# Token sums of three norms and a layer norm through a ones matrix held as weights, with root and inverse over all tokens in PSUM

## The chip, the core and the metric

One Trainium2 chip, one of its cores. A time is the device time of one execution in microseconds (us). The kernel before ran three times: 1002.34, 1003.82 and 1004.71 us, median 1003.82 us.

## What is computed

A decoder trunk of one layer over 512 prompt tokens and 64 sample tokens, 576 in all, with a model width of 1024. Cut to what matters here:

```python
x = x + HALF * gt1 * _swiglu(_rmsnorm(x, g_ffn1) * (1 + sc1) + sh1, w_ffn1_up, w_ffn1_down)      # norm 0
hm = _rmsnorm(x, g_mix) * (1 + scm) + shm                                                        # norm 1
proj = hm @ w_in
...
v = jax.nn.silu(_layernorm(v, ln_g, ln_b))                                                       # layer norm, width 512
...
x = x + gtm * (jnp.concatenate([v, p], axis=-1) @ w_out)
x = x + HALF * gt2 * _swiglu(_rmsnorm(x, g_ffn2) * (1 + sc2) + sh2, w_ffn2_up, w_ffn2_down)      # norm 2
return _rmsnorm(x)                                                                               # final norm

def _rmsnorm(x, g):
    return x * lax.rsqrt(jnp.mean(x * x, axis=-1, keepdims=True) + EPS) * g
```

## The kernel before

Activations lie transposed: 128 channels on the partitions, tokens along a row. `x` has 8 such chunks (`KD`) of 576 tokens (`TOKENS`); a row is treated as two halves of 288 tokens (`HALF`), each half holding 256 prompt and 32 sample tokens, and one half fills part of one PSUM bank. Every product is done in three passes of a value split in a high and a low part (`x_hi`, `x_lo`, `w_hi`, `w_lo`). Weights come in units of 1 MB; ScalarE (ACT) makes the high part of a unit, GpSimd (POOL) the low part, TensorE (PE) multiplies, VectorE (DVE) adds the result to `x`. Every engine's program is written out by hand in the order in which it runs, and semaphores are the only link between them. An instruction that waits holds up all that stands behind it on its engine.

A norm needs, for each token, the sum over 1024 channels of the squares of `x`, its root and inverse, and that inverse in all 128 partitions. Before the change this is done so:

- `square` (L1173) on ACT squares a chunk, `add_square` (L1582, L1585) on DVE adds the first seven into `acc` (a half of the tile `mean_ab`). The eighth square stays by itself in `sq[:, 1, :]`, and in norms 1 and 2 it is made in two halves (`last_square`, L1179 and L1181), since the last output tile of the stage before ends in two halves (`last_tile`, L611, with `last_residual` on DVE, L1877 to L1883, after each half).
- `token_sums` (L823) on PE takes 128 tokens of `acc` or `sq` as weights and one column of ones as the moving operand: 5 matmuls of one column for a row of 576 tokens. The sums of 128 tokens stand down the partitions, in five columns of `stat_ps`.
- `root` (L1222) on ACT and `inverse` (L1589) on DVE work on these 5 columns, in the SBUF tile `rms`.
- `spread` (L831) on PE, called by `norm_spread`, turns each column back into a row and copies it to all partitions (5 transposes of a broadcast column), into `stat_ps`, 576 columns (`r_ps`).
- `apply_norm` on DVE multiplies `x` by it: for each chunk `scale_samples` (L1610), a 512 column product with the gain (L1628) and two small ones. ACT then adds the shift (L1231) and makes `x_hi` (L1235); `x_lo` is made by DVE (L1615, even chunks) and POOL (L2167, odd ones). PE consumes these chunks one by one in `unit_chunk` (L711).

The layer norm is alike: means are taken away on DVE after a ones matmul (`ln_sum`, L977: weights are a 128 by 128 matrix of ones, and the 288 tokens of a half are the moving operand), ACT squares the four chunks of `v` (L1521), DVE adds three (L2119), PE sums (L823), ACT takes the root (L1523), DVE the inverse (L2121), PE spreads, DVE scales `v` (L2124), ACT applies Silu (L1533) and makes `x_hi` (L1529), and PE takes chunks 4 to 7 of unit OUT.

PE's program around these places: at the start a run of 68 transposes without use (`keep_warm`, L894), the sums, `first_products(0)` (L906), the spread, `first_turn(0)` (L915), and then unit 0 chunk by chunk. In norms 1 and 2 the sums of `acc` stand in the middle of the last half tile, the sums of the eighth square after it, with 8 and 6 transposes without use (`fillers`, L839) between, then the spread, then `ada_products` (L561; norm 1 has `ada_turn(4)` too), and the first unit chunk by chunk. In the layer norm the spread stands between chunks 2 and 3 of unit OUT, with `ada_products(7, 0, 1)` behind it.

`ada_products` reads weight quarters that DMA brings; the one that norm 2 waits for is issued by ACT behind the eighth square. On DVE `inverse(n)` stands behind `last_residual`; in norm 1 `mod_evacuate(4)` (L1559, L1572) stands between `inverse` and `apply_norm`. `final_norm` has its own helpers and keeps its own way.

## Time and profile before

| | |
|---|---|
| median of 3 runs | 1003.82 us |
| profiled execution, its own time | 1002.35 us |
| its span | 1000.6 us |
| PE busy | 987.4 us (99%) |
| DVE busy | 666.3 us (67%) |
| ACT busy | 525.4 us (53%) |
| POOL busy | 595.9 us (60%) |
| granted TensorE clock, mean of the span | 0.994 |

The profile is of one execution. The span is the time from the first instruction to the last; the profiled execution took 1.75 us more than its span. A granted clock of 1.00 is 2.4 GHz, of 0.50 it is 1.2 GHz. Matmuls overlap, so the time between the starts of two rows says more than a row's own duration.

### The profile page before, as it was taken

What the parts mean: (1) busy time and instruction counts of PE and PEld (TensorE: products, weight loads), DVE (VectorE), ACT (ScalarE), POOL (GpSimd) and SP (SyncE); (2) the same over time, 40 slices, a digit from 0 to 9 for tenths busy, and PEclk for the clock granted to TensorE, in tenths of its full rate; (3) what the DMA queues carried; (4) which work ended last, traced back from release to release, by engine and by line L of the source; (5) the groups of instructions that cost most, each with busy time, mean ns of one, the idle gap of its engine ahead of it and who ended that gap; (6) DMA issues with size and microseconds to landing.
All of it is one profiled execution on the core that took longest, in us unless ns stands there. A gap on an engine that the chain in (4) does not pass through costs nothing.

```text
span 1000.6 us, 19940 instructions
## 1 busy us (share of the span) xinstructions
PE 987.4 (99%) x7592; PEld 949.6 (95%) x7592; DVE 666.3 (67%) x1341; ACT 525.4 (53%) x957; POOL 595.9 (60%) x497
## 2 busy tenths in 40 slices
PE   8999999999999999999999999999999999999997
PEld 7799999999999998989977898999999999999996
DVE  3787766676666644369996537966776667666464
ACT  5756554556644542373365337656545666455432
POOL 2267666677776563346887133676766777656551
PEclk9999999999999999999999999999999999999998
DMA  9922322232224328744224631232223222232212
GB/s 365 366 86 88 124 84 86 87 123 86 85 86 169 126 85 301 269 164 191 85 34 183 238 127 44 84 110 102 85 85 107 105 86 84 88 124 85 98 72 95
DMA packets 22716, 127.51 MB, mean 127 GB/s; under 512 B 4192, under 2 KB 7392, under 8 KB 8032
## 3 DMA queue, kind: packets, MB, share of 16 engines
q1 hardware_dynamic: 19744, 105.28, 29.2%
q10 hardware_dynamic: 2880, 20.97, 5.5%
q8 instruction: 61, 1.00, 0.4%
q14 instruction: 31, 0.25, 0.1%
HBM read 123.06 MB, written 3.19 MB: 126 GB/s over the span
## 4 chain that ended last, share of the span: by engine, by line
PE 94%; POOL 2%; ACT 1%; DVE 1%; issue 1%; DMA 0%; POOLq 0%; DVEq 0%; ACTq 0%
PE tile_a L736 22%; PE tile_b L736 22%; PE ada_ps L736 18%; PE tile_a L589 10%; PE tile_b L589 8%; PE tile_a L711 2%; PE ada_ps L561 2%; PE tile_b L711 2%; PE tile_b L611 1%; PE tile_a L894 1%; POOL last_taps L2325 1%; PE stat_ps L823 1%; PE ada_ps L906 1%; PE tile_a L963 1%; PE tile_b L648 1%
## 5 line engine op out<-in xcount | busy, mean ns | idle before, releaser
L2181 POOL TENSOR_TENSOR w_lo<-w_raw,w_hi 128x512 fp32r<-128x512 f32 x168 | 217.0, 1298 | 106.7 <-ACT w_hi L1078 106.2
L2181 POOL TENSOR_TENSOR w_lo<-s_raw,w_hi 128x512 fp32r<-128x512 f32 x112 | 146.4, 1308 | 66.7 <-ACT w_hi L1078 66.7
L1078 ACT ACTIVATE w_hi<-w_raw 128x512 fp32r<-128x512 f32 x168 | 104.7, 625 | 63.8 <-PE ada_ps L736 50.2
L2145 POOL TENSOR_TENSOR w_lo<-w_raw,w_hi 128x2048 fp32r<-128x2048 f32 x16 | 73.6, 4597 | 93.6 <-ACT w_hi L1053 90.6
L736 PE MATMUL tile_a<-x_hi,w_hi 128*128 128x288 f32 x400 | 118.5, 296 | 0.0
L736 PE MATMUL tile_b<-x_hi,w_hi 128*128 128x288 f32 x400 | 118.4, 296 | 0.0
L736 PE MATMUL tile_b<-x_lo,w_hi 128*128 128x288 f32 x400 | 118.0, 295 | 0.0
L736 PE MATMUL tile_a<-x_lo,w_hi 128*128 128x288 f32 x400 | 118.0, 295 | 0.0
L736 PE MATMUL tile_b<-x_hi,w_lo 128*128 128x288 f32 x400 | 117.6, 294 | 0.0
L736 PE MATMUL tile_a<-x_hi,w_lo 128*128 128x288 f32 x400 | 117.6, 294 | 0.0
L736 PE MATMUL ada_ps<-x_hi,w_hi 128*128 128x288 f32 x320 | 94.8, 296 | 0.0
L736 PE MATMUL ada_ps<-x_lo,w_hi 128*128 128x288 f32 x320 | 94.4, 295 | 0.0
L736 PE MATMUL ada_ps<-x_hi,w_lo 128*128 128x288 f32 x320 | 94.1, 294 | 0.0
L2219 POOL TENSOR_TENSOR h_lo<-sq,h_hi 128x288 fp32r<-128x288 f32 x64 | 52.9, 847 | 38.3 <-ACT h_hi L1153 38.3
L736 PEld LDWEIGHTS tile_b<-x_hi,w_lo 128*128 128x128 f32 x400 | 75.3, 188 | 0.0
L736 PEld LDWEIGHTS tile_a<-x_hi,w_lo 128*128 128x128 f32 x400 | 75.3, 188 | 0.0
L736 PEld LDWEIGHTS tile_a<-x_lo,w_hi 128*128 128x128 f32 x400 | 75.1, 188 | 0.0
L736 PEld LDWEIGHTS tile_b<-x_lo,w_hi 128*128 128x128 f32 x400 | 75.1, 188 | 0.0
L736 PEld LDWEIGHTS tile_a<-x_hi,w_hi 128*128 128x128 f32 x400 | 74.9, 187 | 0.1
L736 PEld LDWEIGHTS tile_b<-x_hi,w_hi 128*128 128x128 f32 x400 | 74.9, 187 | 0.0
L1078 ACT ACTIVATE w_hi<-s_raw 128x512 fp32r<-128x512 f32 x112 | 70.0, 625 | 1.7 <-PE tile_a L736 1.7
L1125 ACT ACTIVATE full<-ada_ps 128x288 f32<-128x288 f32 x40 | 16.5, 411 | 95.0 <-PE ada_ps L736 95.0
(320 smaller groups left out, 2976.4 us busy)
## 6 DMA issues: line engine op xcount, KB each, us to landing
w_raw<-w_units SPq DMA_DIRECT2D x78, 1024.0 KB, 4.8
ada_lo<-w_ada SPq DMA_DIRECT2D x16, 1024.0 KB, 7.8
ada_lo<-w_ada ACTq DMA_DIRECT2D x14, 1024.0 KB, 7.5
ada_hi<-w_ada ACTq DMA_DIRECT2D x6, 1024.0 KB, 6.1
x<-x_in SPq DMA_DIRECT2D x4, 576.0 KB, 5.9
y_out<-x SPq DMA_DIRECT2D x8, 288.0 KB, 2.3
conv_s<-conv_state SPq DMA_DIRECT2D x1, 480.0 KB, 11.0
conv_s_out<-conv_s SPq DMA_DIRECT2D x1, 480.0 KB, 4.5
```

Source lines behind the costliest of these rows:

```text
L561: mm = pe.matmul(ada_bank(s)[32 * g:32 * g + 32, 0:ADA_N], cond[:, k, :], ada_slot(a)[:, kk, ADA_N * g:ADA_N * (g + 1)], start=(k == 0), s ...
L589: mm = pe.matmul(ps[:, h, 0:HALF], w[:, w_slot, cols], r(k, h), start=(first and n == 0), stop=(last and n == 2))
L611: mm = pe.matmul(tile_b[:, h, 0:HALF], w[:, u % 2, cols], t(k, h), start=(k == 0 and i == 0), stop=(k == kc - 1 and i == 2))
L648: mm = pe.matmul(tile_b[:, h, 0:HALF], w[:, u % 2, cols], t(k, h), start=(k == 0 and i == 0), stop=(k == n - 1 and i == 2))
L711: mm = pe.matmul(tiles[t][:, h, 0:HALF], w[:, u % 2, cols], r(k, h), start=(k == 0 and n == 0), stop=(k == KD - 1 and n == 2))
L736: mm = pe.matmul(ps, slot(w, i)[:, P * k:P * (k + 1)], r, start=(first and n == 0 and k == 0), stop=(n == 2 and k == KH - 1), skip_group_c ...
L823: mm = pe.matmul(out[:, j:j + 1], part[:, begin:begin + P], ones[:, 0:1], start=(first and j == 0), stop=(last and j == TOKEN_BLOCKS - 1))
L1078: nc.scalar.activation(slot(w_hi, i), source, ACT.Copy).then_inc(ready, 1)
L1125: nc.scalar.activation(gate_c22[:, 0, :], bank_a(u), ACT.Silu).then_inc(c11_gate, 1)
L2145: nc.gpsimd.tensor_tensor(w_lo[:, side, :], w_raw[:, side, :], w_hi[:, side, :].bitcast(F32), ALU.subtract).then_inc(w_lo_ready, 1)
L2181: return nc.gpsimd.tensor_tensor(slot(w_lo, i), raw, slot(w_hi, i).bitcast(F32), ALU.subtract)
L2219: nc.gpsimd.tensor_tensor(h_slot(h_lo, kk, x_slot), t1_raw[:, n - 1, :], h_slot(h_hi, kk, x_slot).bitcast(F32), ALU.subtract).then_inc(ht_ ...
```

## The change

`token_sums`, `spread`, `norm_spread` and the tile `rms` go. `row_sums` is new: the weights are the ones matrix, the moving operand is a half row of `acc` or `sq`, and the result is the sum of each of 288 tokens, already in all 128 partitions, in the half's bank of `stat_ps`. The root and the inverse are taken in place there: 288 columns for each half in the norms, 2 by 288 in one instruction in the layer norm. In norms 1 and 2 the sum of the first half of the eighth square stands before the last three matmuls of the last half tile, and its root stands on ACT between the two halves of that square. `column_sums` keeps the 8 fillers and the 6 fillers stay; the final norm stays as it is. Semaphore counts are renumbered for it. The two small slots that `sample_ps` uses move to columns 288 to 415 of their bank.

```diff
@@ last_tile (PE)
                         if h and k == kc // 2:
                             partial_sums(n)
+                        if h and k == kc - 1:
+                            pe.wait_ge(sq_half_ready, n)
+                            row_sums(sq[:, 1, :], 0, False, True).then_inc(stat_done, 1)
@@ partial_sums, column_sums and the helpers (PE)
                 pe.wait_ge(sq_used, (KD - 1) * (n + 1))
-                token_sums(sums_ps, acc, True, False)
+                row_sums(acc, 0, True, False)
+                row_sums(acc, 1, True, False)
 
             def column_sums(n):
                 if n == 0:
                     partial_sums(0)
+                    pe.wait_ge(sq_ready, KD)
+                    row_sums(sq[:, 1, :], 0, False, True).then_inc(stat_done, 1)
                 else:
-                    pe.wait_ge(sq_half_ready, n)
-                    token_sums(sums_ps, sq[:, 1, :], False, False, 0, 2)
                     if n < 3:
                         fillers(n, 8)
-                pe.wait_ge(sq_ready, KD * (n + 1))
-                token_sums(sums_ps, sq[:, 1, :], False, True, 2 if n else 0).then_inc(stat_done, 1)
-
-            def token_sums(out, part, first, last, begin_block=0, end_block=TOKEN_BLOCKS):
-                for j in range(begin_block, end_block):
-                    begin = min(P * j, TOKENS - P)
-                    mm = pe.matmul(out[:, j:j + 1], part[:, begin:begin + P], ones[:, 0:1],
-                                   start=(first and j == 0), stop=(last and j == TOKEN_BLOCKS - 1))
-                return mm
-
-            def spread(out=r_ps):
-                for j in range(TOKEN_BLOCKS):
-                    first = max(0, P * (j + 1) - TOKENS)
-                    mm = pe.transpose(out[:, P * j:P * (j + 1) - first],
-                                      rms[first:, 1, j:j + 1].broadcast_to([P - first, P]), ident[first:, first:])
-                return mm
+                    pe.wait_ge(sq_ready, KD * (n + 1))
+                row_sums(sq[:, 1, :], 1, False, True).then_inc(stat_done, 1)
+
+            def row_sums(part, h, first, last):
+                return pe.matmul(stat_ps[:, h, 0:HALF], ones[:], part[:, HALF * h:HALF * (h + 1)], start=first, stop=last)
...
-            def norm_spread(n):
-                pe.wait_ge(ident_ready, 1)
-                if n in (1, 2):
-                    fillers(n, 6)
-                pe.wait_ge(rstd_ready, n + 1)
-                spread().then_inc(r_ready, 1)
@@ layer norm (PE)
             pe.wait_ge(ln_sq_ready, CONV_CHUNKS)
-            token_sums(sums_ps, four[-1], True, False)
+            row_sums(four[-1], 0, True, False)
+            row_sums(four[-1], 1, True, False)
             ada_products(6, 3)
             pe.wait_ge(ln_sq_added, CONV_CHUNKS - 2)
-            token_sums(sums_ps, acc, False, True).then_inc(ln_var_mm, 1)
+            row_sums(acc, 0, False, True)
+            row_sums(acc, 1, False, True).then_inc(ln_var_mm, 1)
             out_chunk(2)
-            pe.wait_ge(ln_rstd_ready, 1)
-            spread().then_inc(ln_r_ready, 1)
             ada_products(7, 0, 1)
@@ last_square and root (ACT); norm 0 calls root(0, 0) and root(0, 1), norm() calls root(n, 1)
                 nc.scalar.activation(sq[:, 1, 0:HALF], x[:, KD - 1, 0:HALF], ACT.Square).then_inc(sq_half_ready, 1)
+                root(n, 0)
                 act.wait_ge(x_ready, NORM_TILES[n])
...
-            def root(n):
-                act.wait_ge(stat_done, n + 1)
-                nc.scalar.activation(rms[:, 0, :], sums_ps, ACT.Sqrt, scale=1.0 / D_MODEL,
+            def root(n, h):
+                act.wait_ge(stat_done, 2 * n + h + 1)
+                nc.scalar.activation(stat_ps[:, h, 0:HALF], stat_ps[:, h, 0:HALF], ACT.Sqrt, scale=1.0 / D_MODEL,
                                      bias=eps).then_inc(std_ready, 1)
@@ inverse and apply_norm (DVE)
             def inverse(n):
-                dve.wait_ge(std_ready, n + 1)
-                nc.vector.reciprocal(rms[:, 1, :], rms[:, 0, :]).then_inc(rstd_ready, 1)
+                for h in range(2):
+                    dve.wait_ge(std_ready, 2 * n + h + 1)
+                    nc.vector.reciprocal(stat_ps[:, h, 0:HALF], stat_ps[:, h, 0:HALF]).then_inc(rstd_ready, 1)
...
-                dve.wait_ge(r_ready, n + 1)
-                r = by_half(r_ps)
+                dve.wait_ge(rstd_ready, 2 * n + 2)
+                r = rows_ps
@@ layer norm (ACT, then DVE)
-            nc.scalar.activation(rms[:, 0, :], sums_ps, ACT.Sqrt, scale=1.0 / D_CONV, bias=eps).then_inc(ln_std_ready, 1)
+            nc.scalar.activation(rows_ps, rows_ps, ACT.Sqrt, scale=1.0 / D_CONV, bias=eps).then_inc(ln_std_ready, 1)
...
-            nc.vector.reciprocal(rms[:, 1, :], rms[:, 0, :]).then_inc(ln_rstd_ready, 1)
-            dve.wait_ge(ln_r_ready, 1)
+            nc.vector.reciprocal(rows_ps, rows_ps).then_inc(ln_rstd_ready, 1)
+            dve.wait_ge(ln_rstd_ready, 1)
             for c in range(CONV_CHUNKS):
-                nc.vector.tensor_tensor(v[:, c, :], v[:, c, :], r_ps, ALU.mult).then_inc(ln_scaled, 1)
+                nc.vector.tensor_tensor(by_half(v[:, c, :]), by_half(v[:, c, :]), rows_ps, ALU.mult).then_inc(ln_scaled, 1)
```

How the order moves on PE at the end of the first feed-forward stage, where norm 1 begins (`tile_b` is the last half tile, `ones` the ones, `mean_ab` holds `acc`, `ident` the identity). Before:

```order
2643 L611 MATMUL tile_b<-h_hi,w_hi 128x288
2644 L611 MATMUL tile_b<-h_lo,w_hi 128x288
2645 L611 MATMUL tile_b<-h_hi,w_lo 128x288
2646 L823 MATMUL stat_ps<-ones,sq 128x1 x2
2647 L839 MATMUL tile_a<-ident 128x128 x8
2648 L823 MATMUL stat_ps<-ones,sq 128x1 x3
2649 L571 MATMUL ada_ps<-ident,ada_rows 128x128 x2
2650 L839 MATMUL tile_a<-ident 128x128 x6
2651 L831 MATMUL stat_ps<-ident,rms 128x128 x4
2652 L831 MATMUL stat_ps<-ident,rms 128x64
2653 L561 MATMUL ada_ps<-ada_hi,cond 32x256 x8
```

And with the change:

```order
2641 L819 MATMUL stat_ps<-sq,ones 128x288
2642 L610 MATMUL tile_b<-h_hi,w_hi 128x288
2643 L610 MATMUL tile_b<-h_lo,w_hi 128x288
2644 L610 MATMUL tile_b<-h_hi,w_lo 128x288
2645 L825 MATMUL tile_a<-ident 128x128 x8
2646 L819 MATMUL stat_ps<-sq,ones 128x288
2647 L567 MATMUL ada_ps<-ident,ada_rows 128x128 x2
2648 L825 MATMUL tile_a<-ident 128x128 x6
2649 L557 MATMUL ada_ps<-ada_hi,cond 32x256 x8
```

One sum of the eighth square now stands ahead of the last three matmuls of the tile, and no spread stands between the fillers and `ada_products`.

On DVE at the same place, with the instruction behind the inverse (`mod`, `gain` belong to `mod_evacuate(4)`, `stat_ps<-x,stat_ps` is the first of `apply_norm`). Before:

```order
513 L1883 TENSOR_TENSOR x<-tile_b,x 128x32
514 L1589 RECIPROCAL rms<-rms 128x5
515 L1559 TENSOR_TENSOR mod<-ada_ps,vec 128x4x9 x2
516 L1572 SCALAR_TENSOR_TENSOR gain<-mod,vec 128x72
517 L1610 TENSOR_TENSOR stat_ps<-x,stat_ps 128x64
```

With the change:

```order
513 L1865 TENSOR_TENSOR x<-tile_b,x 128x32
514 L1571 RECIPROCAL stat_ps<-stat_ps 128x288 x2
515 L1540 TENSOR_TENSOR mod<-ada_ps,vec 128x4x9 x2
516 L1553 SCALAR_TENSOR_TENSOR gain<-mod,vec 128x72
517 L1592 TENSOR_TENSOR stat_ps<-x,stat_ps 128x64
```

The order is the same; what stands in place 514 is two instructions of 288 columns for one of 5.

## Rows read from the trace of the kernel before

**Rows 1.** The page: busy time by engine, and the chain that ended last
```profile
PE 987.4 (99%) x7592; PEld 949.6 (95%) x7592; DVE 666.3 (67%) x1341; ACT 525.4 (53%) x957; POOL 595.9 (60%) x497
...
PE 94%; POOL 2%; ACT 1%; DVE 1%; issue 1%; DMA 0%; POOLq 0%; DVEq 0%; ACTq 0%
```
**Rows 2.** Instructions on the tiles rms and rms_end: duration in ns, min/median/max
```profile
L1589 DVE RECIPROCAL rms<-rms x3: 189/189/189, 16.2 to 605.1; 128x5 f32<-128x5 f32 x3
...
L1904 DVE RECIPROCAL rms_end<-rms_end x2: 176/177/178, 987.5 to 991.4; 128x3 f32<-128x3 f32 x2
```
**Rows 3.** Groups by line and shape: busy us, mean ns | idle before
```profile
L1125 ACT ACTIVATE full<-ada_ps 128x288 f32<-128x288 f32 x40 | 16.5, 411 | 95.0 <-PE ada_ps L736 95.0
L1760 DVE TENSOR_TENSOR sil<-full,tile_b 128x288 f32<-128x288 f32 x28 | 12.7, 454 | 10.1 <-PE tile_b L736 10.1
```
**Rows 4.** Timeline of PE, layer norm: start us, us, instruction
```profile
532.75 4.10 PE L977 MATMUL stat_ps<-v,ones 128*128 128x288 f32 x16
...
542.77 1.17 PE L823 MATMUL stat_ps<-ones,sq 128*128 128x1 f32 x10
...
547.69 0.80 PE L831 MATMUL stat_ps<-ident,rms 128*128 128x128 f32 x5
...
551.26 0.51 PE L711 MATMUL tile_a<-x_hi,w_hi 128*128 128x288 f32 x2
```
**Rows 5.** Timeline of ACT and DVE, layer norm
```profile
546.19 0.27 ACT L1523 ACTIVATE rms<-stat_ps,small 128x5 f32<-128x5 f32 x1 [4.53 <-PE stat_ps L823]
...
550.22 0.69 ACT L1529 ACTIVATE x_hi<-full 128x576 fp32r<-128x576 f32 x1
...
548.53 2.75 DVE L2124 TENSOR_TENSOR v<-v,stat_ps 128x576 f32<-128x576 f32 x4 [1.85 <-PE stat_ps L831]
```
**Rows 6.** Timeline of norm 1: PE, ACT, DVE
```profile
430.31 0.50 PE L711 MATMUL tile_a<-x_hi,w_hi 128*128 128x288 f32 x2 [0.74 <-ACT x_hi L1235]
...
424.81 0.45 ACT L1181 ACTIVATE sq<-x 128x288 f32<-128x288 f32 x1 [2.82 <-DVE x L1883]
...
424.60 0.18 DVE L1883 TENSOR_TENSOR x<-tile_b,x 128x32 f32<-128x32 f32 x1
...
427.81 0.23 DVE L1610 TENSOR_TENSOR stat_ps<-x,stat_ps 128x64 f32<-128x64 f32 x1 [0.71 <-PE stat_ps L831]
```
**Rows 7.** Norm 2: timeline of PE and DVE, then the chain of waits
```profile
609.30 0.54 PE L711 MATMUL tile_a<-x_hi,w_hi 128*128 128x288 f32 x2
...
603.21 0.18 DVE L1883 TENSOR_TENSOR x<-tile_b,x 128x32 f32<-128x32 f32 x1
...
606.27 0.23 DVE L1610 TENSOR_TENSOR stat_ps<-x,stat_ps 128x64 f32<-128x64 f32 x1 [0.94 <-PE stat_ps L831]
...
603.43 4.82 DMA ada_lo<-w_ada
```
**Rows 8.** Timeline of norm 0, all engines
```profile
15.88 0.25 ACT L1222 ACTIVATE rms<-stat_ps,small 128x5 f32<-128x5 f32 x1
...
18.09 0.23 DVE L1610 TENSOR_TENSOR stat_ps<-x,stat_ps 128x64 f32<-128x64 f32 x1 [1.74 <-PE stat_ps L831]
...
18.80 0.23 DVE L1594 TENSOR_SCALAR mod<-ada_ps,vec 128x9 f32<-128x9 f32 x1 [0.47 <-PE ada_ps L915]
...
21.81 0.53 PE L711 MATMUL tile_a<-x_hi,w_hi 128*128 128x288 f32 x2
```
**Rows 9.** Table by stretch: us, busy (x) of PE, PEld, DVE, ACT, POOL, granted clock, DMA, GB/s
```profile
14.75:15.00 0.25, 0.25 (x6) 0.22 (x9) 0.00 (x0) 0.08 (x1) 0.00 (x0) 0.87 1.08 459
15.00:15.25 0.25, 0.25 (x8) 0.06 (x4) 0.00 (x0) 0.25 (x1) 0.00 (x0) 0.50 1.01 426
...
18.25:18.50 0.25, 0.25 (x3) 0.25 (x4) 0.07 (x1) 0.00 (x0) 0.25 (x2) 0.81 0.98 360
```
**Rows 10.** Timeline of PE in norm 0: the same products at either clock
```profile
14.83 1.89 PE L906 MATMUL ada_ps<-ada_lo,cond 128*32 128x256 f32 x16
...
18.69 1.07 PE L906 MATMUL ada_ps<-ada_lo,cond 128*32 128x256 f32 x16
```

More of the change, by code:

```diff
@@ L252, in trunk @@
         small = sb("small", [P, POOL_PAD + 2])
-        rms = sb("rms", [P, 2, TOKEN_BLOCKS])
         rms_end = sb("rms_end", [P, 2, 2 * HALF_BLOCKS])
@@ L285, in sample_ps @@
         def sample_ps(c):
-            first = TOKENS - 512 + DEC_SEQ * DEC_BATCH * (1 + c % 2)
+            first = HALF + DEC_SEQ * DEC_BATCH * (c % 2)
             return stat_ps[:, 1, first:first + DEC_SEQ * DEC_BATCH].rearrange("p (h n) -> p h n", h=2)
-        r_ps = stat_ps.rearrange("p h n -> p (h n)")[:, 0:TOKENS]
+        rows_ps = stat_ps[:, :, 0:HALF]
         conv_prompt_ps, conv_sample_ps = ada_ps[:, 0, 0:SEQ], ada_ps[:, 1, 0:DEC_BATCH * DEC_SEQ]
@@ L305, in ada_slot @@
             return t.rearrange("p (j n) -> p j n", j=2)
-        sums_ps = stat_ps[:, 1, 512 - TOKEN_BLOCKS:512]
         vec_in, state_in, wp_in = sem("vec_in"), sem("state_in"), sem("wp_in")
@@ L364, in trunk @@
         ln_sq_added = sem("ln_sq_added")
-        ln_std_ready, ln_rstd_ready, ln_r_ready, ln_scaled = (
-            sem("ln_std_ready"), sem("ln_rstd_ready"), sem("ln_r_ready"), sem("ln_scaled"))
+        ln_std_ready, ln_rstd_ready, ln_scaled = sem("ln_std_ready"), sem("ln_rstd_ready"), sem("ln_scaled")
         vmix_full, vmix_hi_ready, vmix_lo_ready = sem("vmix_full"), sem("vmix_hi_ready"), sem("vmix_lo_ready")
@@ L643, in final_tile @@
                         if h and k == n - 1:
-                            pe.wait_ge(rstd_ready, 4)
+                            pe.wait_ge(rstd_ready, 7)
                             final_spread(0, stat_ps).then_inc(r_ready, 1)
@@ L663, in final_norm @@
                 final_fillers(6)
-                pe.wait_ge(rstd_ready, 5)
+                pe.wait_ge(rstd_ready, 8)
                 final_spread(1, stat_ps).then_inc(r_ready, 1)
@@ L927, in _ @@
             first_products(0)
-            norm_spread(0)
             first_turn(0)
@@ L939, in _ @@
             ada_turn(4)
-            norm_spread(1)
+            fillers(1, 6)
             ada_products(5, 0, 2)
@@ L1019, in _ @@
             column_sums(2)
-            norm_spread(2)
+            fillers(2, 6)
             ada_products(8, 1)
@@ L1188, in final_root @@
             def final_root(h):
-                act.wait_ge(stat_done, 4 + h)
+                act.wait_ge(stat_done, 7 + h)
                 blocks = slice(HALF_BLOCKS * h, HALF_BLOCKS * (h + 1))
@@ L1248, in norm @@
             def norm(n, next_unit):
-                root(n)
+                root(n, 1)
                 split_hi(next_unit, first=next_unit < 2)
@@ L1374, in _ @@
             nc.scalar.activation(w_hi[:, 0, 0:UNIT // 2], w_raw[:, 0, 0:UNIT // 2], ACT.Copy).then_inc(w0_half_ready, 1)
-            root(0)
+            root(0, 0)
+            root(0, 1)
             nc.scalar.activation(w_hi[:, 0, UNIT // 2:], w_raw[:, 0, UNIT // 2:], ACT.Copy).then_inc(w_hi_ready, 1)
@@ L1889, in last_residual @@
                         final_inverse(0)
-                        dve.wait_ge(r_ready, 4)
+                        dve.wait_ge(r_ready, 1)
                         scale_out(0, 0, 1)
@@ L1900, in final_inverse @@
             def final_inverse(h):
-                dve.wait_ge(std_ready, 4 + h)
+                dve.wait_ge(std_ready, 7 + h)
                 blocks = slice(HALF_BLOCKS * h, HALF_BLOCKS * (h + 1))
@@ L2136, in _ @@
             scale_out(0, 4, Y_POOL[0])
-            dve.wait_ge(r_ready, 5)
+            dve.wait_ge(r_ready, 2)
             scale_out(1, 0, Y_POOL[0])
```

## The prediction

> **What bounds the kernel now.** I read the page first: PE is busy for 99% of the span, and 94% of the chain that ended last is PE work [rows 1]. So time is won or lost only where PE waits, where it does work that goes, or where its clock falls. The places are the four at which a sum becomes a row: norms 0, 1 and 2 and the layer norm. Then I read the timelines of those places, and last the granted clock. The reader is to see in them that the sums, root, inverse and spread are a short bridge between two stretches of dense matmuls: before norm 1 the first chunk's matmul starts at 430.31 after PE waited 0.74 us for `x_hi` [rows 6], in norm 2 at 609.30 behind a product that DMA had held up [rows 7], in the layer norm chunk 4 starts at 551.26 with no wait [rows 4].
>
> **The prices.** *Sums.* The ones matmul of the layer norm's means is the same instruction as the new one: 8 of them (two records each) in 4.10 us, 0.51 us each [rows 4]. Two of them, 1.02 us, replace 5 matmuls of one column, 1.1 us by starts (10 records, 1.17 us) [rows 4]. That is even: at most 0.1 us is won for each of the 8 pairs. *Spread.* 0.80 us of PE each [rows 4] goes four times; it counts only where PE does not wait afterwards.
>
> *Root.* It grows from 5 to 288 columns: 0.27 us [rows 5] to 0.41 us, by an ACT instruction of the same shape out of PSUM [rows 3]; for 576 columns in one I take 0.65 us, 0.41 plus 288 columns at the slope between these two (0.14 us for 283 columns) and a margin.
>
> *Inverse.* This is the term that decides. No row shows a reciprocal of a row's length. The nearest from below is an ordinary DVE instruction of 288 columns out of PSUM, 0.45 us [rows 3]. But two lengths of the reciprocal itself are there: 3 columns take 0.177 us and 5 take 0.189 us [rows 2]. That is 12 ns for 2 columns, 6 ns a column, where the ordinary instruction pays 0.45 us for 288, at most 1.6 ns a column. At 6 ns a reciprocal of 288 columns takes 0.177 + 285 x 0.006 = 1.89 us and one of 576 takes 3.62 us. The durations scatter by 1 ns, so the slope lies between 5 and 7 ns: 1.60 to 2.17 us, and 3.04 to 4.19 us. I take 6 ns, since the rows are of the same instruction.
> The Trainium skill (VectorE: DVE Perf Modes, the walkthrough's section on the fixed hardware budget) says that a reciprocal is done by iterative divide steps with a repeat count of 8. At one step a cycle of 0.96 GHz (the same skill's clock for VectorE) that would be 8.3 ns a column; as an estimate from that page the two rows should then differ by 17 ns, not 12, so the trace agrees with it on an iterative instruction, not on the factor. By it the sum below would be 5.4 us higher.
>
> **The change place by place** (old starts from the rows; new ones worked out).
>
> *Norm 1.* The half sum put ahead of the last three matmuls makes the tile 0.51 us later, so `last_residual`, which ended at 424.60 + 0.18 [rows 6], ends at 425.3. The first inverse starts there (its root is long done) and ends at 427.1; meanwhile ACT squares the second half (0.45 [rows 6]), PE sums (0.6), ACT takes the root (0.41), done at 426.8, covered by that inverse. The second inverse ends at 429.0. Behind it on DVE stands `mod_evacuate(4)`, three small instructions of the kind that take 0.23 us in rows 8, some 0.5 us with their waits, which used to run during the spread and is now bare. `apply_norm` starts at 429.55 and not at 427.81 [rows 6]: +1.75 us. PE already waited for that chain, so +1.75 us on the path; the spread that goes is only more waiting. PE now waits 2.9 us in place of 0.74.
>
> *Norm 2.* The same without `mod_evacuate`: 603.39 + 0.51, two inverses, 607.65 against 606.27 [rows 7], +1.4 us. PE arrived later than its data here, held by the last `ada_products` quarter, whose DMA is issued behind the square and takes 4.82 us [rows 7]; that gives up 0.5 us of the delay. +0.85 us. PE's waits together are 1.6 us, cut in two by those products.
>
> *Norm 0.* ACT starts the root at 15.88 [rows 8], behind a weight half that DMA sets. Two roots end at 16.3 and 16.6, the inverses at 18.1 and 20.0; `scale_samples` starts at 20.05 for 18.09, and the first `first_modulation` behind it at 20.2 for 18.80 [rows 8]: +1.4 us. The first chunk, 21.81 before, follows it. The spread that goes is followed by a wait for ACT's copy, so it wins nothing.
>
> *Layer norm.* Root 546.05 to 546.7, inverse to 550.4, and DVE scales `v` from there and not from 548.53: +1.9 us. `x_hi` of chunk 4 was done at 550.91 [rows 5], 0.35 us before PE took it at 551.26 [rows 4]; it will be at 552.8, taken at 552.9: +1.65 us. PE, with no spread, arrives at 550.4 and waits 2.5 us.
>
> Sum of the four: 1.75 + 0.85 + 1.4 + 1.65 = 5.65 us. No DMA queue, POOL or SP instruction is added; POOL's part of the next weight unit shifts by some tenths and is not waited for.
>
> *The clock.* The granted clock fell from 1.00 to 0.50 at 14.9 and was back by 18.5 [rows 9], after PE had done the one column sums of norm 0, two runs of ten records. It lies at 1.00 in the whole middle of the span, where no wait of PE is above 0.74 us [rows 6]. Now there are two of 2.9 and 2.5 us. The rows do not show a wait of that length, so below the price is nothing (the clock stays) and above it is a low stretch like the one seen: 3.4 us, in which 16 products took 1.89 us for 1.07 [rows 10], so 1.9 us of work is done and 1.5 us is lost. I take 1.4 us for each of the two, as a part of the stretch can fall on the wait: +2.8 us. Row sums feed the array more than one column sums, so the fall at 14.9 may not come, but nothing there waited on PE's speed.
>
> Total +8.45 us. The profiled execution took 1002.35 us; so 1010.8 us for one like it. It lies 1.5 us under the median of the three, and the forecast is for the median: 1003.82 + 8.45 = **1012.3 us**.
>
> **The rivals.**
>
> 1. *The clock stays up, or falls once.* For it: PE works densely on both sides of each wait. Against: it fell with PE still issuing matmuls. Time 1009.5 us (never) or 1010.9 us (once). The same 1010.9 comes if norm 0's +1.4 is hidden since DMA is the true bound there.
>
> 2. *The reciprocal costs what an ordinary DVE instruction costs*, 0.45 us for 288 columns and 0.75 for 576; the 12 ns are then a quirk of short instructions. It would end on the other side: norm 0 and norm 1 come out even (the second inverse then waits for its root, 427.8 against 427.81), norm 2 costs 0.5 us (DMA is later by it), the layer norm wins 0.9 us since chunk 4 is ready before PE and the spread is really saved. -0.4 us, 1003.4 us. It decides below some 2 ns a column. Against it stand both lengths in rows 2, each seen at least twice within 1 ns.
>
> 3. *The reciprocal costs 8.3 ns a column*: the four places each have 576 columns in line, 1.34 us more each, 1017.7 us. Against: it would show 17 ns between the two lengths. It is the page's factor named above.
>
> 4. *The delays are absorbed.* The data of a chunk are made a little faster than PE takes them, so a late first chunk could be followed by fewer waits at the others: with a third of the 5.65 us given back and the clock up, +3.5 us or so, 1007.3 us (5 ns a column and the clock up give the same, 5.65 - 2.3). Against: PE is the bound after each place, so a delay stays.
>
> **Chances.** Forecast (6 ns, both falls) 0.50; rival 1 0.25; rival 2 0.10; rival 3 0.07; rival 4 0.08. A measurement of this kernel can tell about 0.2%, 2.0 us, from no change. Within it lie 0.08 of rival 2 and 0.02 of rival 4, so 0.10; faster is the rest of rival 2, 0.02; slower is everything else, 0.88. The range runs from rival 4 at 1007.3 us up to the forecast with 7 ns a column (+2.3 us) and one more low stretch (+1.4 us), 1016.0 us.
>
> **What would show it.** RECIPROCAL of 128x288 at 1.6 to 2.2 us, six times, and of 576 columns at 3.0 to 4.2 us; DVE's first `apply_norm` instruction 1.2 to 2 us later against `last_residual`'s start of tile; PE waiting for `x_hi` more than 2 us in norm 1 and the layer norm, and the granted clock at 0.50 for 3.4 us after each. I am wrong if the reciprocal shows at 0.5 us, or if PE's waits stay below 1 us.

## The result, and the profile after

The changed kernel takes 1012.57 us (median of 3 runs, 1011.42 to 1014.0) against 1003.82 us: ratio 1.0083, 95% interval 1.0064 to 1.0102, slower by 6.4 to 10.2 us. The forecast was 1012.3 us, 1007.3 to 1016.0. The profiled execution is the one of 1012.57 us, with a span of 1010.8 us, 10.2 us over that of before. So the total was met, but not by its parts: several were off and cancelled, which is luck (the table in the part on the prediction has them).

The page, busy time by engine and the chain that ended last, answers to [rows 1]:

```profile
PE 987.1 (98%) x7524; PEld 946.9 (94%) x7524; DVE 681.9 (67%) x1344; ACT 528.1 (52%) x960; POOL 595.2 (59%) x497
...
PE 92%; DVE 3%; ACT 2%; POOL 1%; DMA 1%; issue 1%; SPq 0%; DVEq 0%; POOLq 0%; ACTq 0%
```

PE is busy for the same time, but it is only 92% of the chain, and VectorE has become 3% of it. The inverses, by line (duration in ns, minimum/median/maximum), answer to [rows 2]:

```profile
L1571 DVE RECIPROCAL stat_ps<-stat_ps x6: 1904/1962/1967, 16.1 to 615.8; 128x288 f32<-128x288 f32 x6
...
L2103 DVE RECIPROCAL stat_ps<-stat_ps x1: 3767/3767/3767, 555.2 to 555.2; 128x576 f32<-128x576 f32 x1
```

From 3 columns (178 ns here) to 288 that is 1784 ns for 285 columns, 6.3 ns each; to 576 columns, 6.3 ns each. Where PE waits (waits of PE: us in total, times, longest):

```profile
PE tile_a L710 <- ACT x_hi L1215: 5.2, 2, 4.6
PE ada_ps L894 <- ACT ada_rows L1350: 2.9, 3, 1.9
PE tile_a L710 <- ACT x_hi L1510: 2.4, 1, 2.4
```

The 4.6 us are norm 1's (forecast 2.9), the 2.4 the layer norm's (2.5). The timeline of norm 1, VectorE, GpSimd and the first chunk, answers to [rows 6]:

```profile
428.52 3.88 DVE L1571 RECIPROCAL stat_ps<-stat_ps 128x288 f32<-128x288 f32 x2
...
432.30 2.34 POOL L2136 TENSOR_TENSOR w_lo<-w_raw,w_hi 128x1024 fp32r<-128x1024 f32 x1 [9.54 <-ACT w_hi L1031]
432.31 0.23 DVE L1540 TENSOR_TENSOR mod<-ada_ps,vec 128x36 f32<-128x36 f32 x2
432.57 2.16 DVE L1553 SCALAR_TENSOR_TENSOR gain<-mod,vec 128x72 f32<-128x72 f32 x1
434.76 0.23 DVE L1592 TENSOR_TENSOR stat_ps<-x,stat_ps 128x64 f32<-128x64 f32 x1
...
437.25 0.50 PE L710 MATMUL tile_a<-x_hi,w_hi 128*128 128x288 f32 x2 [4.63 <-ACT x_hi L1215]
```

A VectorE instruction over 72 columns takes 2.16 us and ends with GpSimd's `w_lo`. The two `mod` instructions ahead of it, with one input out of PSUM (`ada_ps`), took 0.23 us together beside the same `w_lo`. The same `gain` took 0.23 us before:

```profile
426.87 0.23 DVE L1572 SCALAR_TENSOR_TENSOR gain<-mod,vec 128x72 f32<-128x72 f32 x1
...
428.32 2.38 POOL L2154 TENSOR_TENSOR w_lo<-w_raw,w_hi 128x1024 fp32r<-128x1024 f32 x1 [9.04 <-ACT w_hi L1053]
```

There it was done before `w_lo` began. Layer norm and norm 2, the rows that answer to [rows 4, 5, 7]:

```profile
555.19 3.77 DVE L2103 RECIPROCAL stat_ps<-stat_ps 128x576 f32<-128x576 f32 x1 [4.76 <-ACT stat_ps L1504]
...
558.99 2.75 DVE L2106 TENSOR_TENSOR v<-v,stat_ps 128x576 f32<-128x576 f32 x4
...
561.42 0.53 PE L710 MATMUL tile_a<-x_hi,w_hi 128*128 128x288 f32 x2 [2.40 <-ACT x_hi L1510]
...
617.80 0.23 DVE L1592 TENSOR_TENSOR stat_ps<-x,stat_ps 128x64 f32<-128x64 f32 x1
...
620.29 0.50 PE L710 MATMUL tile_a<-x_hi,w_hi 128*128 128x288 f32 x2 [0.60 <-ACT x_hi L1215]
```

And the granted clock (stretch, its length, busy time of PE, PEld, DVE, ACT and POOL, clock, DMA share, GB/s):

```profile
17.75:18.00 0.25, 0.23 (x2) 0.23 (x2) 0.25 (x2) 0.00 (x0) 0.25 (x1) 0.85 1.09 459
18.00:18.25 0.25, 0.25 (x3) 0.25 (x2) 0.25 (x2) 0.00 (x0) 0.25 (x2) 0.50 0.94 393
...
28.00:28.25 0.25, 0.25 (x8) 0.10 (x4) 0.25 (x2) 0.00 (x0) 0.00 (x0) 0.67 0.18 66
...
437.75:438.00 0.25, 0.25 (x4) 0.25 (x3) 0.25 (x2) 0.24 (x1) 0.00 (x0) 0.53 0.92 197
441.00:441.25 0.25, 0.25 (x4) 0.25 (x3) 0.25 (x1) 0.25 (x1) 0.00 (x0) 0.65 0.82 229
...
561.00:565.00 4.00, 3.58 (x27) 3.59 (x28) 2.82 (x5) 3.94 (x6) 0.00 (x0) 1.00 0.87 332
```

It is at 0.50, which is 1.2 GHz where 1.00 is 2.4 GHz, for 10.2 us in norm 0 (3.4 before, from 14.9), for 3.4 us in norm 1, and not at all in the layer norm. In the final norm it is low in both, for the last 6.4 us of the span and the last 9.4 before.

To see where the time came from I cut the span at PE's first matmuls of norm 1's sums, of the layer norm's means, of norm 2's sums and of the final norm's sums. The table gives each stage in us, with the time for which the clock was low in it behind a slash. The slash is left out for the end, where the clock was low in every profiled execution: the end takes 13.7 to 13.8 us with 4.0 to 6.8 us of low clock, 14.1 with some 7.6, and 14.8 with 9.4. All runs below are read by this table.

| profiled kernel | norm 0 on | norm 1 on | layer norm on | norm 2 on | end | span |
|---|---|---|---|---|---|---|
| before | 421.6 / 3.4 | 111.15 | 67.05 | 385.9 | 14.8 | 1000.6 |
| changed | 425.1 / 10.2 | 115.9 / 3.4 | 69.0 | 387.0 | 13.8 | 1010.8 |
| change_again | 424.7 / 6.8 | 115.9 / 3.4 | 69.3 | 387.0 | 14.1 | 1011.0 |
| short_inverse | 422.5 / 3.4 | 111.7 | 66.2 | 386.5 | 14.1 | 1000.9 |
| mod_between | 424.5 / 6.8 | 112.7 | 68.9 | 387.1 | 14.1 | 1007.2 |
| warm | 423.5 / 0 | 114.6 | 70.5 / 3.4 | 387.1 | 13.8 | 1009.4 |
| warm_between | 423.8 / 0 | 112.9 | 68.9 | 387.0 | 13.8 | 1006.4 |
| one_step | 424.1 / 6.8 | 111.7 | 66.2 | 386.3 | 13.7 | 1002.1 |
| one_step_warm | 421.9 / 0 | 111.6 | 66.3 | 386.2 | 13.7 | 999.7 |
| ln_rows | 424.4 / 10.2 | 111.1 | 70.3 / 3.4 | 385.9 | 13.7 | 1005.4 |
| hybrid | 424.2 / 10.2 | 111.1 | 66.2 | 386.0 | 13.7 | 1001.2 |
| hybrid_warm | 422.1 / 0 | 111.15 | 66.3 | 386.0 | 13.7 | 999.2 |
| before_warm | 421.6 / 0 | 111.2 | 68.6 / 3.4 | 385.9 | 13.8 | 1001.0 |
| before_mod_late | 422.8 / 3.4 | 116.7 / 6.8 | 68.5 / 3.4 | 386.0 | 14.1 | 1008.1 |

### The profile page after: what moved, and what is told of

Read it like the earlier page. It is cut to its first block, busy times and chain, and to the rows that moved or that the text cites. A ratio compares the mean times of both kernels' runs of the same rounds, so it can differ in the third digit from the quotient of the medians.

```text
span 1010.8 us, 19807 instructions
## 1 busy us (share of the span) xinstructions
PE 987.1 (98%) x7524; PEld 946.9 (94%) x7524; DVE 681.9 (67%) x1344; ACT 528.1 (52%) x960; POOL 595.2 (59%) x497
## 4 chain that ended last, share of the span: by engine, by line
PE 92%; DVE 3%; ACT 2%; POOL 1%; DMA 1%; issue 1%; SPq 0%; DVEq 0%; POOLq 0%; ACTq 0%
PE tile_b L735 22%; PE tile_a L735 22%; PE ada_ps L735 18%; PE tile_a L585 10%; PE tile_b L585 8%; PE tile_a L710 3%; PE tile_b L710 2%; PE ada_ps L557 2%; PE tile_b L610 1%; DMA w_raw<-w_units 1%; PE ada_ps L885 1%; POOL last_taps L2307 1%; DVE stat_ps L1571 1%; PE tile_a L941 1%; PE tile_b L647 1%
```

## Experiments: what the inverse costs

**short_inverse**, the inverse cut to three columns in all places:

```diff
-                    nc.vector.reciprocal(stat_ps[:, h, 0:HALF], stat_ps[:, h, 0:HALF]).then_inc(rstd_ready, 1)
+                    nc.vector.reciprocal(stat_ps[:, h, 0:3], stat_ps[:, h, 0:3]).then_inc(rstd_ready, 1)
...
-            nc.vector.reciprocal(rows_ps, rows_ps).then_inc(ln_rstd_ready, 1)
+            nc.vector.reciprocal(stat_ps[:, 0, 0:3], stat_ps[:, 0, 0:3]).then_inc(ln_rstd_ready, 1)
```

> The changed kernel with each RECIPROCAL over the row sums cut to 3 columns of its row; the inverse is left out for all other columns. Everything else of the change stays (sums by the ones matrix, wide roots, no spread). If the wide inverse is what the change costs: each of the seven wide instructions takes about 0.18 us, norm 0's low clock is back near 3.4 us (10.24 us in the changed kernel), VectorE's gain in norm 1 is back at 0.23 us (2.16), and the time is 1003 to 1004.5 us, that of the kernel before. If sums of 576 columns and roots of 288 and 576 carry a good part of it: 1006 to 1009 us.

Measured: 1003.85 us beside 1004.4 for before, ratio 0.9992 (0.9979 to 1.0005). The inverses by line (duration in ns):

```profile
L1571 DVE RECIPROCAL stat_ps<-stat_ps x6: 179/190/190, 16.3 to 606.1; 128x3 f32<-128x3 f32 x6
```

And the gain behind them in the timeline of norm 1:

```profile
428.20 0.23 DVE L1553 SCALAR_TENSOR_TENSOR gain<-mod,vec 128x72 f32<-128x72 f32 x1
```

The whole slowdown is gone with the width of one instruction. What is left of the change is about even: the layer norm's stage is 0.8 us shorter than before, norms 1 and 2 are 0.5 us longer each, and norm 0 is 0.9 us longer with 3.4 us of low clock in both (the end, 0.7 us shorter, is the clock's).

**one_step** keeps the computation whole and takes the inverse away: root and inverse are one activation, in the norms, the layer norm and the final norm. In the norms:

```diff
-                nc.scalar.activation(stat_ps[:, h, 0:HALF], stat_ps[:, h, 0:HALF], ACT.Sqrt, scale=1.0 / D_MODEL,
+                nc.scalar.activation(stat_ps[:, h, 0:HALF], stat_ps[:, h, 0:HALF], ACT.Abs_reciprocal_sqrt, scale=1.0 / D_MODEL,
...
-                for h in range(2):
-                    dve.wait_ge(std_ready, 2 * n + h + 1)
-                    nc.vector.reciprocal(stat_ps[:, h, 0:HALF], stat_ps[:, h, 0:HALF]).then_inc(rstd_ready, 1)
+                dve.wait_ge(std_ready, 2 * n + 2)
```

> The changed kernel with root and inverse in one activation, Abs_reciprocal_sqrt on ScalarE, and no RECIPROCAL on VectorE. If one column of any activation costs the same, its 288 columns take 0.47 us as the root does, and the time is that of the short inverse less a handoff and 0.18 us at each of four places: 1002 to 1003.5 us, at or just below the kernel before. If the function is dearer than the root or calls for more table loads: 1005 us or more.

Measured: 1004.08 us, ratio 0.9996 (0.9985 to 1.0006). The activation takes what the root took, 477 ns against 476, and the table loads are as many as in the changed kernel (9 at the line of the roots, 1 elsewhere):

```profile
L1202 ACT ACTIVATE stat_ps<-stat_ps,small x6: 457/477/478, 16.1 to 607.4; 128x288 f32<-128x288 f32 x6
```

That is 0.6 us above what I expected, and not told apart from short_inverse. The handoff that I wanted to save was not there to save: in norm 1 `scale_samples` starts 1.11 us after the last root's start, 1.18 us in short_inverse. In the profiled executions norm 0 lost the clock for 6.8 us here and for 3.4 in short_inverse, and is 1.7 us longer here.

**ln_rows**, the layer norm's part of the change alone in the kernel before:

```diff
-            token_sums(sums_ps, acc, False, True).then_inc(ln_var_mm, 1)
+            row_sums(acc, 0, False, True)
+            row_sums(acc, 1, False, True).then_inc(ln_var_mm, 1)
...
-            spread().then_inc(ln_r_ready, 1)
...
-            nc.vector.reciprocal(rms[:, 1, :], rms[:, 0, :]).then_inc(ln_rstd_ready, 1)
+            nc.vector.reciprocal(rows_ps, rows_ps).then_inc(ln_rstd_ready, 1)
```

> The kernel before with the layer norm's part of the change alone: row sums by the ones matrix, root and inverse over 576 columns, no spread there; the three norms as before. If places add up: the layer norm's 1.9 us of the changed kernel's stages, so 1005.0 to 1006.3 us, all of it between TensorE's first matmul of the layer norm's sums and norm 2. If the layer norm's delay is mostly absorbed once the norms don't delay it, less than 0.7 us: 1003.8 to 1004.5.

Measured: 1005.84 us beside 1004.29, ratio 1.0008 (0.9997 to 1.002): neither expectation is excluded, as the interval reaches from -0.3 to +2.0 us. The profiled execution has the stage 3.2 us longer, of which 1.3 us is a fall of the clock that the changed kernel, with a wait of the same 2.4 us, did not have. The layer norm as it was before, which has no such wait, lost the clock in two of the profiles below (before_mod_late, before_warm), so this fall is not shown to be the wait's.

## Experiments: the gain beside GpSimd

**mod_between**:

```diff
                 for h in range(2):
+                    if n == 1 and h == 1:
+                        mod_evacuate(4)
                     dve.wait_ge(std_ready, 2 * n + h + 1)
                     nc.vector.reciprocal(stat_ps[:, h, 0:HALF], stat_ps[:, h, 0:HALF]).then_inc(rstd_ready, 1)
...
-            mod_evacuate(4)
             apply_norm(1)
```

> The changed kernel with one edit: in norm 1, VectorE issues the three small instructions of mod_evacuate(4) between the two inverses instead of behind them, so that its gain (SCALAR_TENSOR_TENSOR, 2.16 us in the changed kernel) runs before GpSimd's w_lo begins. If it was long because w_lo ran beside it: it takes about 0.23 us, and the time falls by 1.7 to 2.2 us, to 1010.4 to 1010.9. If it was long for a reason of VectorE's own (it stands right behind an inverse, or waits in its pipeline for it): it stays at about 2 us there too, and the time moves by less than 0.5 us.

Measured: 1008.83 us, ratio 1.0049 (1.0033 to 1.0065), 3.4 us under the changed kernel's ratio and more than I expected. The timeline of norm 1:

```profile
430.01 0.23 DVE L1553 SCALAR_TENSOR_TENSOR gain<-mod,vec 128x72 f32<-128x72 f32 x1
430.28 1.97 DVE L1573 RECIPROCAL stat_ps<-stat_ps 128x288 f32<-128x288 f32 x1
431.66 2.36 POOL L2137 TENSOR_TENSOR w_lo<-w_raw,w_hi 128x1024 fp32r<-128x1024 f32 x1 [9.54 <-ACT w_hi L1031]
...
434.78 0.50 PE L710 MATMUL tile_a<-x_hi,w_hi 128*128 128x288 f32 x2 [2.79 <-ACT x_hi L1215]
```

Behind an inverse and the two `mod` instructions, as in the changed kernel, but ahead of `w_lo`, the gain takes 0.23 us. The second inverse, out of PSUM, takes its usual 1.97 us though `w_lo` starts inside it. PE's wait falls from 4.63 to 2.79 us, and with it the low clock of norm 1 is gone: 3.2 us for that stage, 1.9 of them the gain's (2.16 less 0.23) and 1.3 left for the clock, which is also what warm, below, gives for it. Another 0.6 us of the profiled execution is norm 0, with 6.8 us of low clock for 10.2.

**before_mod_late** brings the collision into the kernel before, which has no wide inverse:

```diff
+            dve.wait_ge(w_hi_ready, MIX + 2)
             mod_evacuate(4)
             apply_norm(1)
```

> The kernel before with one wait added: in norm 1, VectorE begins mod_evacuate(4) only when ScalarE's w_hi is done, which is what GpSimd's w_lo waits for too. There is no wide inverse in it. If a VectorE instruction with both inputs in SBUF can't run beside GpSimd's: the gain (SCALAR_TENSOR_TENSOR, 0.23 us before) takes 1.9 to 2.2 us, until w_lo ends, and norm 1 ends 2.5 to 3 us later: 1006.5 to 1007.5 us. If it was the inverses in front of it that made it long in the changed kernel: 0.23 us, and norm 1 ends 0.9 us later, 1004.5 to 1005.

Measured: 1009.22 us beside 1004.69, ratio 1.0051 (1.0033 to 1.0068). The timeline of norm 1:

```profile
429.56 2.35 POOL L2155 TENSOR_TENSOR w_lo<-w_raw,w_hi 128x1024 fp32r<-128x1024 f32 x1 [9.05 <-ACT w_hi L1053]
429.85 2.16 DVE L1572 SCALAR_TENSOR_TENSOR gain<-mod,vec 128x72 f32<-128x72 f32 x1
432.04 0.23 DVE L1610 TENSOR_TENSOR stat_ps<-x,stat_ps 128x64 f32<-128x64 f32 x1
...
434.53 0.82 PE L711 MATMUL tile_a<-x_hi,w_hi 128*128 128x288 f32 x2 [3.72 <-ACT x_hi L1235]
```

The gain started 0.3 us behind `w_lo` and was held until that was done. The inverses have no part in it. PE's first chunk is 3.0 us later against the stage's start; the other 2.5 us of the stage come with 6.8 us of low clock. The layer norm lost 1.5 us too, with 3.4 us of low clock. I had expected neither, and the time is above my bound. The Trainium skill (SBUF — State Buffer, the section on who interferes with whom) says that a VectorE instruction with two SBUF inputs contends with a GpSimd instruction that reads SBUF. The same page of the Trainium skill (the section on the two separate sides) adds that whichever starts first has the shared ports for its whole length and the other is blocked. Gain reads `mod` and `vec`, `w_lo` reads `w_raw` and `w_hi`, all in SBUF; the runs agree, with 2.16 us for the gain that came second against 0.23 for the one that came first.

## Experiments: the clock

**warm** fills PE's waits in norms 0 and 1 with transposes that nothing reads:

```diff
             first_products(0)
+            keep_warm(0, 12)
...
                 first_products(c)
+                if c in (1, 2):
+                    keep_warm(0, 4)
...
             fillers(1, 6)
+            fillers(1, 30)
```

> The changed kernel with transposes that nothing reads in TensorE's waits: 12 behind the first ada_products and 4 behind each of the next two in norm 0, 30 behind norm 1's six ones. If the low clock (10.24 us in norm 0, 3.4 us in norm 1) costs what the rows say, about 1.4 us and 1.5 us: the granted clock stays at 1.00 through both norms and the time falls by 1.5 to 3 us, to 1009.5 to 1011. If the stretches at low clock are covered by VectorE's chain, which sets the pace of the tiles there: clock up all the same, and the time within 0.7 us of the changed kernel's.

Measured: 1011.05 us, ratio 1.0064 (1.0049 to 1.008), 1.5 us under the changed kernel and at the upper edge of what I expected. The clock stayed up in both norms, for 1.6 us in norm 0's stage and 1.3 us in norm 1's. But now it fell in the layer norm, at the wait of 2.40 us at which the changed kernel kept it (table by stretch, the clock is the first number behind the brackets):

```profile
556.00:560.00 4.00, 1.60 (x9) 1.60 (x9) 3.52 (x6) 3.17 (x5) 0.00 (x0) 0.86 0.92 387
560.00:564.00 4.00, 4.00 (x24) 4.00 (x23) 2.35 (x5) 2.73 (x4) 0.00 (x0) 0.72 0.77 272
```

That took 1.5 us back.

**warm_between** has both edits, that of mod_between (here behind the wait for the second root) and those of warm:

```diff
+            fillers(1, 30)
...
+                    if n == 1 and h == 1:
+                        mod_evacuate(4)
```

> The changed kernel with both edits at once: mod_evacuate(4) between the inverses, and the transposes in TensorE's waits of norms 0 and 1. By the stages of the two kernels alone, norm 0 gives what it gave in warm (1.6 us less than the changed kernel), norm 1 what it gave in mod_between (3.2 us less). If these are two causes and the clock's part of norm 1 is counted once: 1012.6 - 1.6 - 3.2 = 1007.8 us, 1007 to 1009. If the layer norm's wait loses the clock here, as it did in warm, 1.5 us more: 1009.3. What then stays over the kernel before is the bare chain of roots and inverses. If the sums were simply additive over whole kernels (3.7 and 1.5 us): 1007.4, which this run can't tell from the first.

Measured: 1009.28 us beside 1004.29, ratio 1.0047 (1.0032 to 1.0061), just above the 1007 to 1009 that I expected with the clock up in the layer norm. The profiled execution, at 1008.18 us, lies within that: it has no low clock outside the final norm and a mean granted clock of 0.997. Four of the six, from 1009.24 to 1010.4 us, have 0.995, which is an estimated 4 us more of low clock (0.002 of 1007 us, twice); where it fell in them no trace shows. So the profiled one shows the bare price of the four bridges, against before_warm where that is up: norm 0 +2.2, norm 1 +1.7, norm 2 +1.1, and against before the layer norm +1.9 us. By the times it is not told apart from mod_between.

**change_again**, the changed kernel once more:

> The changed kernel once more, in more rounds and beside the runs of this call. The ratio to the kernel before stands within 1.0064 to 1.0102. Of the granted clock: if the low stretch of norm 0 (10.24 us in its first profile) is the change's own, it is 10.24 us again; if it varies from one execution to the next, as the kernels with the norms as before show (3.4 us in the profile of before, 10.24 in two others with the same norm 0), it may be 3.4 or 6.8 us, and the time up to norm 1's sums differs by about 0.2 us for each us.

Measured: 1011.88 us beside 1004.69, ratio 1.0077 (1.006 to 1.0094). The low stretch of norm 0 was 6.8 us this time. And two kernels whose norm 0 is word for word that of before differ from its profile, which has 3.4 us from 14.9 on: before_mod_late has 3.4 us from about 21 on, and ln_rows has 10.2 us from about 16 on (table by stretch):

```profile
16.00:18.00 2.00, 1.64 (x11) 1.15 (x7) 0.33 (x2) 1.28 (x3) 2.00 (x1) 0.55 1.05 430
18.00:20.00 2.00, 2.00 (x19) 1.27 (x20) 1.24 (x5) 0.00 (x0) 2.00 (x2) 0.50 0.98 340
20.00:24.00 4.00, 3.50 (x29) 1.56 (x21) 1.94 (x8) 1.68 (x3) 0.66 (x1) 0.50 0.92 332
24.00:28.00 4.00, 4.00 (x36) 3.59 (x32) 1.38 (x7) 1.68 (x3) 1.41 (x1) 0.70 0.91 328
```

So that stretch is not the change's own; it varies by execution. (Of the "two others" in the expectation one, hybrid, has another activation in its norm 0.)

**before_warm** puts transposes into norm 0 of the kernel before:

```diff
                     partial_sums(0)
+                    keep_warm(0, 8)
...
             first_products(0)
+            keep_warm(0, 6)
             norm_spread(0)
...
                 first_products(c)
+                if c in (1, 2):
+                    keep_warm(0, 4)
```

> The kernel before with the transposes of hybrid_warm in norm 0 and nothing else. If norm 0's low clock varies between executions of the kernel before (3.4 to 10.24 us) and costs up to 2 us there, its median should fall by 0.5 to 1.5 us against before, to 1002.8 to 1003.8, with the clock up in the whole of norm 0. If what varies between executions (1002.2 to 1007.1 in 28 runs of before) is not the clock of norm 0: the same scatter, and the median within 0.5 us of before's.

Measured: 1002.8 us beside 1004.69, ratio 0.9981 (0.997 to 0.9992). Its 12 runs lie between 1001.43 and 1003.4, 2 us apart; the 23 of before between 1002.14 and 1008.23, 6 us apart. The time goes with the clock: the runs of before up to 1002.52 us have a mean granted clock of 0.995, those above 1006 us one of 0.987 to 0.989. With norm 0 filled most of this scatter is gone here, so most of it is norm 0's clock. Hybrid_warm, below, scatters by 6 us with the same filling, so this is shown for this kernel alone.

## Experiments: a version that beats both

**hybrid** is the kernel before with the one-step activation in the norms (5 columns and spread kept) and the change's layer norm without its inverse; **hybrid_warm** adds the transposes of before_warm. In the norms and in the layer norm of hybrid:

```diff
-                nc.scalar.activation(rms[:, 0, :], sums_ps, ACT.Sqrt, scale=1.0 / D_MODEL,
+                nc.scalar.activation(rms[:, 1, :], sums_ps, ACT.Abs_reciprocal_sqrt, scale=1.0 / D_MODEL,
...
-            nc.scalar.activation(rms[:, 0, :], sums_ps, ACT.Sqrt, scale=1.0 / D_CONV, bias=eps).then_inc(ln_std_ready, 1)
+            nc.scalar.activation(rows_ps, rows_ps, ACT.Abs_reciprocal_sqrt, scale=1.0 / D_CONV, bias=eps).then_inc(ln_std_ready, 1)
```

> A version of both: the kernel before with root and inverse in one activation (Abs_reciprocal_sqrt, no RECIPROCAL) in all norms, spread and 5 columns as before, but the layer norm by the change's row sums without a spread. In one_step the layer norm's stage took 0.8 us less than before, and taking a RECIPROCAL of 0.19 us and its handoff out of three norms should give about 0.3 us each: 1001.6 to 1002.6 us, faster than both kernels. If the reciprocals of the norms are hidden behind something else: 1003.0, hard to tell from before.

> The version of both, with transposes that nothing reads in TensorE's waits of norm 0 (8 between the two sums, 6 ahead of the spread, 4 behind each of two products), where the kernel before loses the clock for 3.4 us. If that stretch costs TensorE about 0.5 us there (0.16 us for each us at low clock, from the changed kernel against warm): 0.3 to 0.8 us under hybrid, 1001 to 1002 us. If the transposes delay the spread by as much as the clock gives: no difference from hybrid.

Measured: 1003.15 us, ratio 0.9984 (0.9972 to 0.9996), and 1002.88 us, ratio 0.9985 (0.9971 to 0.9998), beside 1004.29. Both beat before by a little, and both are above what I expected (1001.6 to 1002.6, and 1001 to 1002 us). Hybrid's norms 1 and 2 take what they took before (111.1 and 386.0 us), so an inverse of 5 columns and its handoff are hidden there, and the gain is the layer norm's 0.8 us. Hybrid_warm, though its norm 0 is filled, scatters over 6 us (11 runs from 1000.42 us at a mean clock of 0.997 to 1006.42 at 0.990); where the clock fell in the slow ones no trace shows. The medians don't tell the two apart; the profiled executions do, by 2.0 us in norm 0 (10.2 us of low clock and none).

**one_step_warm** is one_step with warm's transposes in norm 0:

```diff
             first_products(0)
+            keep_warm(0, 12)
```

> The change's own form at its best: root and inverse in one activation, row sums and no spread everywhere, with the transposes of warm in norm 0. One_step lost the clock for 6.8 us in norm 0, which by 0.16 to 0.2 us for each us is 1.1 to 1.4 us: 1002.5 to 1003.2 us, just below before. If the row sums are worth as much as 5 columns with a spread once the inverse is gone, this stands level with hybrid_warm (1002.9); if they cost more in the three norms, 0.5 to 1.5 us above it.

Measured: 1001.58 us beside 1004.69, ratio 0.997 (0.9957 to 0.9984), 12 runs from 1000.83 to 1002.9: 3.1 us under before, the lowest median of all and lower than I expected. Its ratio's interval overlaps hybrid_warm's, and the two profiled executions are 0.6 us apart (999.7 and 999.2 us). The change's own form, without its inverse and with the clock kept, is as good as 5 columns and a spread.

## Why the prediction was right, and where it was not

The sum of the prediction against the stages, in us of the profiled executions:

| term | predicted | shown |
|---|---|---|
| norm 0, clock up | +1.4 | +2.2 (warm_between against before_warm; warm: +1.9) |
| norm 1, clock up, no collision | +1.75 | +1.5 (mod_between) |
| layer norm, clock up | +1.65 | +1.9 |
| norm 2 | +0.85 | +1.1 |
| gain held by `w_lo` | none | +1.9 |
| clock, norm 1 | +1.4 | +1.3 |
| clock, layer norm | +1.4 | 0 in both profiles of the changed kernel, 1.3 to 1.5 where it fell |
| clock, norm 0 | none | +1.3 (the stage's 3.5 less 2.2; by warm 1.6) |
| clock, final norm | none | -1.0 |
| sum | +8.45 | +10.2 |

*The inverse.* Right, and it is the term that decides: 6.3 ns a column where I took 6, from two short rows. By my estimate from the Trainium skill (VectorE: DVE Perf Modes, the walkthrough's section on the fixed hardware budget) it would be 8.3 ns; 1.96 us for 288 columns instead of 2.5 says no, as the short rows did.

*The root* was short by 0.06 us of 0.41 (0.476) and by 0.07 of 0.65 (0.715). It was hidden in the norms and is in the layer norm's +1.9.

*"Three small instructions of the kind that take 0.23 us"*, the step on `mod_evacuate(4)`, failed. I asked what was moved past on VectorE's own queue, 0.5 us, and not what runs beside it where it lands: it came to stand under GpSimd's `w_lo`, and one of the three took 2.16 us. The two extra microseconds also took PE's wait in norm 1 from 2.8 to 4.6 us, and in mod_between, where it is 2.79, the clock stayed up. So the clock's 1.3 us there hung on the collision, in the executions seen.

*The clock.* The price of a fall between dense matmuls was right: 1.3 to 1.5 us for 3.4 us at 0.50 in norm 1 and the layer norm, 1.4 predicted. The places were not. I put one fall to each wait over 2 us; the same wait of 2.40 us lost the clock in warm and ln_rows and kept it in four profiles (the changed kernel's two, mod_between, warm_between), and the layer norm of before lost it in before_warm and before_mod_late without such a wait. What decides it stays open. And *"nothing there waited on PE's speed"* holds for the stretch from 14.9 that I had seen (norm 0 takes 421.6 us in before and in before_warm) and not for one that reaches into the chunks: 10.2 us at the low clock cost 1.3 to 1.6 us in the changed kernel and 2.0 in hybrid against hybrid_warm. The first row of the table rests on kernels whose clock is up, since the two first profiles differ by luck there.

*The base.* The profiled execution of before, at 1002.35 us, is among its fastest; beside the later kernels its medians are 1004.3 to 1004.7. The difference of the two spans, 10.2 us, is therefore larger than that of the medians, 8.75 and 7.2 us in two measurements. I added the sum to the median, which was the right base for a forecast of a median. That 1012.3 came within 0.3 us of 1012.57 is luck all the same: the terms above are off by up to 1.9 us one way and 1.4 us the other, and the second measurement of the difference is 1.3 us under the sum.

Rival 2 said what is left with a cheap inverse: 1003.4 us, the layer norm ahead by 0.9 us and norm 2 behind by 0.5. short_inverse gave 0.8 and 0.5 and a ratio of 0.9992; only norm 1 was not even but 0.5 us behind, and norm 0 by 0.9 (0.4 with the clock up, one_step_warm against before_warm). That the slowdown turns on the price of one instruction is shown.

In norm 0 the forecast of +1.4 us was right for what it was made for, the first chunk. The timeline of warm_between has it at 23.23, 1.4 us behind the 21.81 of before [rows 8], and the third chunk at 30.09; before, that stood at 28.55, 1.5 us earlier:

```profile
28.55 0.53 PE L711 MATMUL tile_a<-x_hi,w_hi 128*128 128x288 f32 x2
```

```profile
23.23 0.50 PE L710 MATMUL tile_a<-x_hi,w_hi 128*128 128x288 f32 x2 [0.39 <-ACT x_hi L1219]
...
30.09 0.53 PE L710 MATMUL tile_a<-x_hi,w_hi 128*128 128x288 f32 x2
...
47.75 1.07 PE L557 MATMUL ada_ps<-ada_lo,cond 128*32 128x256 f32 x16 [0.41 <-DMA ada_lo<-w_ada]
```

The other 0.6 us come in the `ada_products` behind that unit, where PE waits 0.41 us for a weight quarter from DMA (0.29 in warm). The sum had no term for that. The changed kernel does not wait there: by the low clock its third chunk starts at 32.04, 1.9 us behind warm_between, and at norm 1's sums 1.3 us of that are left.

## What to carry to other kernels

A statistic should go through its dear per-element step while it is narrow; widening it first (576 columns for 5) came out even here only with that step cut short or taken away, and two short rows of the instruction were enough to tell that it was dear. When an instruction moves in time, look at what the other engines run at its new place, above all GpSimd when VectorE reads two operands from SBUF. And where executions of one kernel scatter, look at the clock of its thin stretches before comparing two single profiles.

## What I had not expected of the hardware

- VectorE's gain over 72 columns: 0.23 us alone, 2.16 us when it starts 0.3 us behind GpSimd's `w_lo` of 2.35 us, in two kernels with nothing else in common there.
- The same norm 0 had its low clock for 3.4 us, 3.4 us elsewhere and 10.2 us in the profiled executions of before, before_mod_late and ln_rows, and the changed one for 10.2 and 6.8 us in two.
- In before_warm the clock fell for 3.4 us in the layer norm, at 546.4, behind the one column sums (from 542.8 to 546.0) and with no wait of PE. It did the same in before_mod_late, at 553.3 behind the same sums, and not in before. In before_warm, by stretch:

```profile
544.00:548.00 4.00, 4.00 (x36) 3.42 (x33) 0.19 (x1) 1.79 (x4) 2.77 (x1) 0.80 1.02 424
548.00:552.00 4.00, 4.00 (x33) 3.00 (x33) 1.95 (x3) 1.37 (x3) 0.00 (x0) 0.77 1.00 422
```

- `Abs_reciprocal_sqrt` over 288 columns takes 0.477 us, the time of `Sqrt`, and needed no more table loads than `Sqrt` did.
